# Reversed gate chunks, identity products as plain matmuls, and a new expert pipeline in a two-model fp32 kernel

## The reference

```
for e in range(32):                                  # top 2 of 32 experts per token
    y[e] = (silu(x[e] @ w_gate[e]) * (x[e] @ w_up[e])) @ w_down[e]   # 1024 -> 512 -> 1024

def _wkv_step(S, inp):                               # 16 heads, 2 directions, 64 x 64 state
    r_t, w_t, k_t, v_t, a_t, b_t = inp
    sa = jnp.einsum('zbhvk,zbhk->zbhv', S, a_t)
    S = S * w_t[..., None, :] + sa[..., :, None] * b_t[..., None, :] + v_t[..., :, None] * k_t[..., None, :]
    return S, jnp.einsum('zbhvk,zbhk->zbhv', S, r_t)
```

## Time and profile before

| what | us |
|---|---|
| median of three runs | 4901.6 (4897.2 to 4904.73) |
| profiled execution, span | 4899.6 |
| PE busy | 4236.2 (86%) |
| DVE busy | 1338.8 (27%) |
| ACT busy | 474.8 (10%) |
| POOL busy | 351.2 (7%) |

### The profile page before, as it was taken

The page is one execution under the profiler, slowest core; times in us unless marked ns, Lnnn a source line. Parts: engine busy times, 40 slices in busy tenths (PEclk is TensorE's granted clock), DMA queues, the critical chain, the costliest instruction groups (busy, mean ns, idle before and its releaser), DMA issues. The chain is left out here.

```text
span 4899.6 us, 68797 instructions
## 1 busy us (share of the span) xinstructions
PE 4236.2 (86%) x28873; PEld 3247.8 (66%) x28873; DVE 1338.8 (27%) x2979; ACT 474.8 (10%) x844; POOL 351.2 (7%) x471
## 2 busy tenths in 40 slices
PE   7996699989993999998497888898898885999996
PEld 6774368875542777776244776786687774777775
DVE  4533635414104000000423333423433322000001
ACT  1002210011001000000101101110110100000001
POOL 0000000000001000000001021112102100000000
PEclk9978569889695899999697555555555556999998
DMA  6732027612112899998110000000000013999995
GB/s 220 232 115 71 1 70 251 203 51 87 35 60 66 256 306 307 307 307 288 52 58 12 1 1 1 2 1 1 2 1 1 1 62 109 300 309 304 311 304 171
DMA packets 547008, 641.48 MB, mean 131 GB/s; under 512 B 26905, under 2 KB 442185, under 8 KB 546425
## 3 DMA queue, kind: packets, MB, share of 16 engines
q1 hardware_dynamic: 507460, 543.65, 34.8%
q10 hardware_dynamic: 31926, 71.73, 4.0%
q0 software_dynamic: 7424, 23.12, 1.7%
HBM read 611.67 MB, written 26.77 MB: 130 GB/s over the span
## 5 line engine op out<-in xcount | busy, mean ns | idle before, releaser
L1560 PEld LDWEIGHTS bank<-ex_xt,weights 128*128 128x128 f32 x8192 | 945.6, 196 | 52.6 <-issue 52.6
L1560 PE MATMUL bank<-ex_xt,weights 128*128 128x64 f32 x8192 | 954.4, 280 | 1.9 <-DVE ex_xt L1612 1.9
L1575 PE MATMUL bank<-weights,ex_hidden 128*64 128x512 f32 x1024 | 457.6, 600 | 4.3 <-DVE ex_hidden L1617 1.4
L394 PE MATMUL bank<-u,weights 128*128 128x272 f32 (+1 forms) x1408 | 318.0, 389 | 16.6 <-DVEq L415 16.6
L1575 PEld LDWEIGHTS bank<-weights,ex_hidden 128*64 128x64 f32 x1024 | 136.0, 138 | 278.3 <-issue 265.2
L394 PEld LDWEIGHTS bank<-u,weights 128*128 128x128 f32 x1408 | 270.3, 192 | 64.3 <-DVEq L415 17.4
L1617 DVE TENSOR_TENSOR ex_hidden<-ex_silu,bank 128x128 f32<-128x128 f32 x128 | 36.8, 288 | 906.8 <-ACT ex_silu L1593 906.8
L2333 PE MATMUL bank<-sc_xt,sc_bt 64*64 64x64 f32 x2560 | 259.4, 314 | 0.0
L2333 PEld LDWEIGHTS bank<-sc_x,sc_n 64*64 64x64 f32 x2560 | 231.9, 220 | 37.4 <-issue 37.4
L2333 PEld LDWEIGHTS bank<-sc_xt,sc_bt 64*64 64x64 f32 x2560 | 245.9, 220 | 0.0
L2333 PE MATMUL bank<-sc_x,sc_n 64*64 64x64 f32 x2560 | 239.4, 314 | 1.0 <-PEq L2253 1.0
(11 more groups left out here) (499 smaller groups left out, 4628.8 us busy)
## 6 DMA issues: line engine op xcount, KB each, us to landing
weights<-in_moe_w_gate_dram SPq DMA_DIRECT2D x128, 1024.0 KB, 5.4
weights<-in_moe_w_up_dram SPq DMA_DIRECT2D x128, 1024.0 KB, 8.0
weights<-in_moe_w_down_dram SPq DMA_DIRECT2D x128, 1024.0 KB, 8.1
ada_w<-in_ada_w_dram ACTq DMA_DIRECT2D x24, 2048.0 KB, 8.7
weights<-in_w_gate_dram SPq DMA_DIRECT2D x22, 1024.0 KB, 5.8
weights<-in_w_up_dram SPq DMA_DIRECT2D x22, 1024.0 KB, 8.2
weights<-in_w_down_dram SPq DMA_DIRECT2D x32, 704.0 KB, 6.7
weights<-in_ga_w_in_dram SPq DMA_DIRECT2D x16, 1024.0 KB, 5.6
```

Of the source, the lines that this page charges most:

```text
L394: last = nc.tensor.matmul(k.bank[b + side * NB][:, 0:N], w[:, f, c * P:(c + 1) * P], rhs[:, f, 0:N], start=(f == 0), stop=(f == DC - 1))
L1560: last = nc.tensor.matmul(k.bank[2 + q][:, o:o + SLOTS], w[:, f * 256 + c * P:f * 256 + (c + 1) * P], xt[:, s, f * SLOTS:(f + 1) * SLOTS], ...
L1575: last = nc.tensor.matmul(k.bank[4 + 2 * s + n][0:SLOTS, :], hid[:, s, f * SLOTS:(f + 1) * SLOTS], w[:, f * 512:(f + 1) * 512], start=(f = ...
```

## The change

It has these parts:
1. `gate_up_stage` sums the eight chunks of its reduction from the last to the first.
2. The four users of Ln and Exp load one table that holds both, once and ahead of the wait. In the whole program the ACT_TABLE_LOAD rows go from 49 to 30.
3. The first feed-forward's modulation sums are no block any more: 14 columns each are summed in the norms `fqn` and `fkn`, 10 each in `cq` and `ckv`, into bank 7. The four norms stand ahead of the allocation of q and k. The second's sums stay a block.
4. The overflow rows are cleared in `attention_stage`, by one memset on GpSimd and three stores on SP.
5. `ExpertRing`: 18 slots of 1 MB in place of six, so that loads are three experts ahead; the first three experts are asked for in `route_stage`, on SP behind the router's weights. A piece of gate or up is half of the 1024 reduction rows in full width, 8 KB in one run per partition; a piece of down is two rows of 4 KB per partition. Token rows are stored in a matching order, on ACT's queue. The projections' weights are asked for when the second expert from the end has been computed.
6. `experts_stage` is written out without a loop. The 64 slots are the stationary operand and 256 columns of weights move; the two halves of the columns go to PSUM partitions 0 to 63 and 64 to 127. Two transposes turn the hidden values, and the down products put their two halves in the same two places. One VectorE copy of 128x512 takes the result out, and two stores write it.
7. In `scan_matrices` all identity products are ordinary matmuls. In `blocks_matmul` the loops over chunk and row half change places.
8. In `scan_states` ScalarE makes both copies of direction 1, VectorE those of direction 0, with a semaphore for each direction.

The diff, cut to its core:

```diff
+    def place(self, k, ctx):
+        more = [ctx.enter_context(k.nc.sbuf_tensor(f"expert_weights_{k.name_count()}_{s}", [P, 2048], F32, side="right"))
+                for s in range(self.SLOTS - RING)]
+        self.slots = [s[:, 0:2048] for s in k.stream.slots] + [s[:, :] for s in more]
+        self.need = {}
+
+    def start(self, sp, a, l, e, j):
+
+        s = (self.PIECES * e + j) % self.SLOTS
+        if j < 4:
+            w = a["moe_w_gate_2" if j % 2 == 0 else "moe_w_up_2"][l, e]
+            src = w.rearrange("(p k) m -> p (k m)", k=DC)[:, (j // 2) * 2048:(j // 2) * 2048 + 2048]
+            sp.dma_start(self.slots[s], src).then_inc(self.landed[s], 16)
+        else:
+            w = a["moe_w_down_2"][l, e]
+            src = w.rearrange("(k p) m -> p k m", p=P)[:, (j - 4) * 2:(j - 4) * 2 + 2, :]
+            sp.dma_start(self.slots[s].rearrange("p (k m) -> p k m", k=2), src).then_inc(self.landed[s], 16)
+        self.count[s] += 16
+        self.need[e, j] = self.count[s]
...
+            if mods is not None:
+                mods.sums(10)
...
-                        for f in range(DC):
+                        for f in reversed(range(DC)):
                             last = nc.tensor.matmul(k.bank[b + side * NB][:, 0:N], w[:, f, c * P:(c + 1) * P],
-                                                    rhs[:, f, 0:N], start=(f == 0), stop=(f == DC - 1))
+                                                    rhs[:, f, 0:N], start=(f == DC - 1), stop=(f == 0))
...
+    def sums(self, count):
+
+        nc = self.k.nc
+        for m in range(self.columns, self.columns + count):
+            for v in range(2):
+                last = nc.tensor.matmul(self.k.bank[7][:, 2 * m + v:2 * m + v + 1],
+                                        self.acc[:, v, m * P:(m + 1) * P], self.k.ones[:, 0:1], start=True, stop=True)
+        self.columns += count
+        last.then_inc(self.summed, 1)
+        self.parts += 1
...
+            for e in range(3):
+                for j in range(k.ring.PIECES):
+                    k.ring.start(sp, a, l, e, j)
...
+            for e in range(3, NE):
+                for j in range(ring.PIECES):
+                    sp.wait_ge(spent, 4 * (e - 3) + (1, 1, 2, 2, 3, 4)[j])
+                    ring.start(sp, k.a, l, e, j)
+            if l == 0:
+                sp.wait_ge(spent, 4 * (NE - 2) + 4)
+                k.stream.resume(sp, k.seg["wo"].first)
...
+                    ring.wait(pe, e, 2 * j)
+                    ring.wait(pe, e, 2 * j + 1)
+                    for q in range(4):
+                        f = 4 * j + q
+                        for side in range(2):
+                            w = ring.slot(e, 2 * j + side)
+                            for t in range(2):
+                                last = nc.tensor.matmul(half_cols(k.bank[2 + side], t),
                                                         xt[:, s, f * SLOTS:(f + 1) * SLOTS],
+                                                        w[:, q * 512 + t * 256:q * 512 + t * 256 + 256],
                                                         start=(f == 0), stop=(f == DC - 1))
...
+                if e + 1 < NE:
+                    turn(e + 1)
+                pe.wait_ge(gated, e + 1)
+                for c in range(2):
+                    last = nc.tensor.transpose(k.bank[4][:, c * P:(c + 1) * P], hid[:, s, c * P:(c + 1) * P],
+                                               k.ident[:, :])
+                last.then_inc(hturned, 1)
+                pe.wait_ge(hcopied, e + 1)
+                if e >= 2:
+                    pe.wait_ge(kept, e - 1)
+                for j in range(2):
+                    ring.wait(pe, e, 4 + j)
+                    w = ring.slot(e, 4 + j)
+                    for q in range(2):
+                        o = q * P + j * RH
+                        for n in range(2):
+                            last = nc.tensor.matmul(k.bank[6 + s][n * RH:(n + 1) * RH, :], ht[:, s, o:o + SLOTS],
+                                                    w[:, q * D + n * 512:q * D + n * 512 + 512],
+                                                    start=(j == 0 and q == 0), stop=(j == 1 and q == 1))
                     last.then_inc(spent, 1)
...
                         elif ops[1] is None:
                             src = ops[0][rows, t] if kind == "vt" else ops[0][rows, z, t]
-                            if h == 0:
-                                last = nc.tensor.transpose(to, src, k.ident[rows, rows])
-                            else:
-
-                                last = nc.tensor.matmul(to, src, k.ident[rows, rows], start=True, stop=True)
+                            last = nc.tensor.matmul(to, src, k.ident[rows, rows], start=True, stop=True)
...
 def blocks_matmul(nc, ps, lhsT, rhs):
 
-    for h in HALVES:
-        rows = slice(h, h + RH)
-        for j in range(NCH):
-            t = slice(j * CH, (j + 1) * CH)
+    for j in range(NCH):
+        t = slice(j * CH, (j + 1) * CH)
+        for h in HALVES:
+            rows = slice(h, h + RH)
             last = nc.tensor.matmul(ps[rows, t], lhsT[rows, t], rhs[rows, t], start=True, stop=True)
...
+        def _(act):
+            for i in range(NCH):
+                act.wait_ge(rmade, 2 * i + 2)
+                nc.scalar.activation(rs[1][:, :], k.bank[1][:, 0:RH], ACT.Copy).then_inc(rkept[1], 1)
+                act.wait_ge(samade, 2 * i + 2)
+                solved_free(act, i, 1)
+                nc.scalar.activation(sa[1][:, :], k.bank[1][:, RH:2 * RH], ACT.Copy).then_inc(sakept[1], 1)
```

More of the change, by code:

```diff
@@ L339, in _ @@
                                                    op0=ALU.mult, op1=ALU.mult).then_inc(ready, 1)
+            if mods is not None and mods.columns == 6 * DC:
+                mods.spread(dve)
             if parts[0][3] is not None:
@@ L996, in ffn @@
-def ffn(k, n, h, u, T, t0, seg, gains, to):
+                self.sums(6 * DC)
+            block.vector(self.spread)
+def ffn(k, n, h, u, T, t0, seg, gains, to, acc):
     nc = k.nc
@@ L1571, in expert @@
-                for n in range(2):
-                    k.stream.wait(pe, seg, e, 4 + n)
-                    w = k.stream.slot(seg, 4 + n)
-                    for f in range(4):
-                        last = nc.tensor.matmul(k.bank[4 + 2 * s + n][0:SLOTS, :], hid[:, s, f * SLOTS:(f + 1) * SLOTS],
-                                                w[:, f * 512:(f + 1) * 512], start=(f == 0), stop=(f == 3))
+                if e + 1 < NE:
+                    turn(e + 1)
+                pe.wait_ge(gated, e + 1)
@@ L1635, in overflow_stage @@
         sb = lambda n, s, dt=F32: ctx.enter_context(nc.sbuf_tensor(f"ov{l}_{n}", s, dt))
-        w = [sb(f"w{n}", [P, 2048]) for n in range(6)]
+        w = k.ring.slots[RING:RING + 6]
         idx = sb("idx", [SLOTS, 1], I32)
@@ L1835, in moe @@
         norm_stage(k, f"moe_norm{l}", k.x, DC, D, EPS, parts, hm)
+        more = ExitStack()
+        k.ring.place(k, more)
         route_stage(k, l, hm, T, rows, slot_token, table, dest, desti, wts, out_rows)
```

321 lines of the change are left out of this document (155 added, 166 removed).

## The result

| | before | after |
|---|---|---|
| median, us | 4903.1 (4 runs) | 3962.5 (3961.3 to 3968.2, 4 runs) |
| span of the profiled execution | 4899.6 | 3959.6 |
| ratio | | 0.8084, 95% interval 0.8073 to 0.8096 |

A forecast was written before the change was run, and what follows sets the result against it. PE and DMA, both near their limits, bound the expert stages, and small PE products at half clock the scan's inversion. Experts -374, scan -464, sums -30, tables -14 make -882 from 4899.6: 4020 us, range 3880 to 4260.

The forecast's parts named there:

- Experts: Both expert stages: DMA-limited at 18.2 us an expert, PE 12.9; -191 us in layer 0, -183 in layer 1, sum -374.
- Rival 3: Expert stages: longer runs don't help the DMA, 20.9 us an expert; +150, 4170 us; chance 0.07.
- Rival 1: Expert stages: the column halves don't run at once, PE needs 23.6 us an expert; 4460 us; chance 0.11.
- The inversion: Scan, `blocks_matmul`: 28 calls go from 74 to 28 us, mostly at full clock; block at 56 us, -39 a round.
- PEclk near 1.0 with PE busy about 60%: Scan's inversion: the sign that the forecast is right; a clock of 0.50 would point to rival 2.
- The scan: Eight rounds: inversion -39, identity products -16.7, states -1, output -1.3, together -58 a round, -464 us in all.
- Identity products: Scan, ahead of the inversion: as plain matmuls they end before GpSimd's last mask; -16.7 us a round (-12 to -19).
- States: Scan states: direction 1's copies leave VectorE's queue for ScalarE; -1 us a round (+3 to -4).
- Sums: Modulation sums: a 41 us stretch goes beside four norms, which lengthen a little; -30 us (bounds -41, 0).
- Tables: Ten norms: one table load of 1.28 us leaves each chain; -14 us (bounds 0, -20).
- rival 2: Scan: inversion stays at 1.2 GHz or stalls on copies, 28 us a round, states as now; +110, 4130; chance 0.13.
- Rival 5: Unrolled expert stages wait for their code; 5040 us at 30 us a packet, 5720 at 50; chance 0.02.

The follow-up runs named there:

- experiment 7: Changed kernel with the load pieces of the kernel before (runs of 1 KB for gate and up, 2 KB for down), ring of 18 kept: 4123.2 us.
- experiment 6: Changed kernel with both column halves of the experts' products sent to PSUM partitions 0 to 63: 4458.8 us.
- Experiments 1 and 2: 1: changed kernel with `blocks_matmul` alone as before, 4294.2 us; 2: kernel before with `blocks_matmul` alone taking row halves by turns, 4569.5 us.
- experiments 7 to 10: Changed kernel; 8: no expert weights asked for in router, 4023.9 us; 10: layer 1's norm asks router weights, then ten pieces, 19 slots, 3953.7 us; 7, 9 separately.
- experiment 4: Changed kernel with all four copies of a state step on VectorE: 3960.5 us.
- experiment 5: Changed kernel with gate and up summing their eight chunks from first to last again: 3958.0 us.
- experiment 11: Changed kernel without the four loads of the joint Ln and Exp table, each function loading its own: 3976.9 us.
- experiment 9: Changed kernel with layer 1's first ten expert weight pieces asked for in the norm ahead of the router: 3962.8 us.

## Why the prediction was right, and where it was off

**Experts (-374 forecast, -405 measured with the router).** The mechanism was right in each part: PE 12.45 us an expert where 12.9 was forecast, DMA as the limit (from the eighth expert on), the slot table of layer 1 later by 11 us where 8 were forecast. The mis-sized term is the DMA period, 18.2 us against 17.35. The rate was 392 GB/s where I had 404, so queue time was 17.7 us rather than 17.3; but I had divided by a share of 0.95 taken from the earlier trace rows, and the share became 1.02. A DMA share beside a busy PE said what the loads were given, not what they could take: with one expert ahead they had to wait for slots. That is 0.85 x 29 = 25 us a stage. 8 of them went back: the first slots come free 2 us later than I had, and from there 29 x 17.35 end at 2059, 10.5 us before the last copy ends where I had 4.

Rival 3 (short runs) was priced +150, and experiment 7 measured +161. Rival 1 was priced 4460, and experiment 6 measured 4458.8, but that they meet is in part luck: by the profiled executions the two expert stages with layer 1's router grew by 90 us over the kernel before, not 70, and everything else saved 530, not 508.

**The inversion (-39, measured -40 a round; -49 in the last).** The forecast for the calls themselves (28 x 1.0) can be read in the last round, where no preparation is in between: 27.9 us, against 76.7 before. With preparation it is 52.8, near the forecast of 56, and that is in part luck. The sign that I had named, PEclk near 1.0 with PE busy about 60%, did not come: the clock is 0.81, and PE is busy 41.8 us (76% of the window), where 28 us of calls and 5 to 10 of LoRA products make 33 to 38. The idle time, for which the forecast had left some 18 to 23 us, is 11. The term "full clock for most of it" was set too high, the waits too long. Experiments 1 and 2 show 332 and 335 us with both heads of a call in one bank. By the rule of the Trainium skill (TensorEngine Tiling (Array Packing), Gotcha 1: PSUM Pressure) that row tiles cannot access one bank at the same time there would have been no gain; the measurement decides against that conclusion for these products. The two heads of a call also write different partitions of the bank; products that differ in their rows alone are not measured here.

The scan came out 34 us below its forecast. The seven other rounds gave 59.3 us each, not 58 (mean period 172.2 to 112.9): 9 us. The last round, which I had counted like the others, gave 67.4 from its first mask to its states and 5.6 behind them: 15 us more than 58. Its inversion ran at full clock without a pause. Its states then took 23.3 us, not 27.1, and these 4 us are luck of the clock: 1.00 in that execution, about 0.6 and 27.9 us in those of experiments 7 to 10, whose last rounds run the same code. 6 us are a side effect that I had not listed: in the kernel before, SP also asked for the first pieces of layer 1's experts directly behind the output projection's weights. PE began 11.8 us after SP's first issue there, and begins 5.8 us after it now. In both traces PE's first product comes 0.6 us after SP's last issue (4023.6 and 3281.0), and before, the two issues of expert pieces took 2.9 us each, while the first weights had landed at 4017.5. That fits a stage's end that waits for SP; no run tests it alone. The last 4 us lie in the stages ahead of the scan (2.3) and behind it (2.0, of which one table load is 1.3).

**Identity products** -16.7, measured -17.5 (mean of seven rounds; -18.4 against the round of the earlier trace rows): GpSimd's chain is the end of the stage, as forecast, and it began earlier relative to PE's jobs.

**States** -1, measured 0 for the exchange of the copies (experiment 4): the copy takes 0.22 us on either engine, and the chain is products and hand-overs. The states did get 0.9 us a round shorter, but through the clock: 24.0 us in every second round. **Order of the gate's chunks** 0, measured 0 (experiment 5). **Sums** -30, measured -24 (medians) to -26 (trace): at 213 ns a record, 40 records take 8.5 us, and the way from the start of `cq` to that of `ckv` grew from 7.2 us to 11.3. **Tables** -14 in the norms: experiment 11 measures 14 in all, but that the two figures meet is luck. By the traces, 11 us apart, some 10 are norms; the last round has 6, of which 4 go with the clock, and the other rounds and layer 1's router give part of it back. Those in the scan gave 1.3 us a round as forecast, and the preload in the preparation lost as much on balance: 3.1 us in the inversion, of which the states gave 1.3 back (experiment 11).

In the prediction's own working, rival 2's terms (11 us of the inversion and 1 of the states, in eight rounds) make 96 us, not 110. That changes none of its ranges.

**Rival 5** (code loading) did not show: the fetches grew from 2.72 to 3.33 MB in 203 packets, and in 300 us of the experts 12 packets went by while the DMA share was 1.02. PE's waits there were for weights and, for about 0.5 us at a time, for the hidden values.

## What to carry to other kernels

Small products that use half of the array's rows and columns, or half of its columns, should take turns between the halves, also into one PSUM bank: in the inversion that alone took 335 of 4900 us, and its opposite in the experts cost 496. Of a stream of loads ask three things apart: how long a contiguous run is (325 or 392 GB/s here), whether the queue ever pauses for buffers, and what small transfers stand behind it in the same queue. The share of DMA time beside a busy engine is no measure of what the loads can reach. And before a difference of a few microseconds in one stage is put down to an edit, look at the granted clock in it: the same states took 24.0 and 26.9 us in one execution.

## What the runs showed that I had not expected

- A sustained DMA share of 1.01 to 1.02 at 388 to 394 GB/s over whole expert stages, 3 MB of gathers and stores in each hundred microseconds among them.
- Once the head start has filled the ring, the DMA engines have next to nothing to do: some 34 us until the first slot comes free.
- Loads asked for early delay what stands behind them in the queue: an SP issue of 10.87 us, and the router's first product 13 us later in its stage (experiment 9).
- A table load ahead of time in work that runs beside the inversion gave nothing: 112.6 us a round without, 112.9 with.
